# Expert tiles of an encoder block: the order of wide and narrow products, and the place of one wait

## The reference

```
q   = (xb @ w_query).reshape(TB, PH, 2, PEER_QUERY_DIM // 2)
s   = einsum('thpd,hpkd->thpk', q, sub_keys)      # top 16 of 128 keys, twice, for 8 heads
idx, g = best 16 of the 16 x 16 pairs, and their softmax
u = expert_u[idx]
a = gelu(einsum('td,thkd->thk', xb, u))
return einsum('thk,thkd->td', g * a, expert_v[idx])
```

## Time and profile before

| | us |
|---|---|
| median of 3 runs | 932.35 (932.03 to 935.43) |
| the profiled execution | 932.16 |
| its span, first to last instruction | 930.3 |
| TensorE busy (matmul) | 923.0 (99%) |
| TensorE weight loads | 879.0 (94%) |
| DVE / ACT / GpSimd busy | 799.1 / 576.2 / 373.4 |

### The profile page before, as it was taken

One profiled execution on the slowest core, in us unless ns is written; L12 is line 12 of the kernel. 1 busy time (PEld: TensorE's weight loads), 2 busy tenths in 40 slices (PEclk: granted clock), 3 DMA queues, 4 the chain that ended last, 5 costly groups with the idle time before them and its releaser, 6 DMA issues.

```text
span 930.3 us, 20125 instructions
## 1 busy us (share of the span) xinstructions
PE 923.0 (99%) x6652; PEld 879.0 (94%) x6652; DVE 799.1 (86%) x1613; ACT 576.2 (62%) x1069; POOL 373.4 (40%) x222
## 2 busy tenths in 40 slices
PE   9999999999999999999999999999999999999997
PEld 9999889999999999999999999999999999999997
DVE  7988877887799997888989976788998898989886
ACT  6555764655746646888888776655555555555555
POOL 0000000047697787888877877121121222123200
PEclk9999999999999999999999999999999999999999
DMA  8877658666587897999999999999999999999981
GB/s 303 265 232 230 204 179 245 199 223 214 160 246 241 228 258 199 263 287 279 238 258 278 236 245 256 303 387 380 364 358 368 370 382 352 365 356 359 378 276 46
DMA packets 135828, 256.04 MB, mean 275 GB/s; under 512 B 30964, under 2 KB 79988, under 8 KB 135500
## 3 DMA queue, kind: packets, MB, share of 16 engines
q1 hardware_dynamic: 110508, 226.72, 73.7%
q0 software_dynamic: 24816, 27.60, 12.3%
q10 hardware_dynamic: 432, 0.80, 0.3%
HBM read 229.17 MB, written 25.85 MB: 274 GB/s over the span
## 4 chain that ended last, share of the span: by engine, by line
PE 94%; DVE 3%; issue 1%; ACT 1%; DMA 1%; DVEq 0%; ACTq 0%
PE pOO L1524 29%; PE pOO L1532 8%; PE pMM L1532 8%; PE pTT L1836 6%; PE pOO L1836 6%; PE pMM L1836 6%; PE pSS L1836 6%; PE pOO L1533 4%; PE pMM L1533 4%; PE pTT L1837 3%; PE pOO L1837 3%; PE pMM L1837 3%; PE pSS L1837 3%; DVE wlos L975 1%; PE pSS L1598 1%
## 5 line engine op out<-in xcount | busy, mean ns | idle before, releaser
L695 ACT ACTIVATE whis<-raw 128x1024 fp32r<-128x1024 f32 x326 | 343.7, 1056 | 157.5 <-PE pSS L1837 115.9
L670 POOL DMA_INDIRECT g_scratch<-small x117 | 211.4, 1807 | 51.2 <-issue 33.5
L1524 PE MATMUL pOO<-xpair,whis 128*128 128x232 f32 (+1 forms) x1184 | 205.9, 277 | 0.0
L975 DVE TENSOR_TENSOR wlos<-raw,whis 128x1024 fp32r<-128x1024 f32 x155 | 188.2, 1218 | 11.4 <-ACT whis L695 10.4
L1412 DVE TENSOR_TENSOR wlos<-raw,whis 128x1024 fp32r<-128x1024 f32 x125 | 152.9, 1223 | 38.3 <-ACT whis L695 38.0
L1524 PEld LDWEIGHTS pOO<-xpair,whis 128*128 128x128 f32 x1184 | 179.9, 190 | 1.4 <-issue 1.3
L1524 PE MATMUL pOO<-xpair,wlos 128*128 128x232 f32 (+1 forms) x592 | 163.2, 276 | 0.0
L635 POOL TENSOR_TENSOR wlos<-raw,whis 128x1024 fp32r<-128x1024 f32 x30 | 72.0, 2408 | 214.7 <-ACT whis L695 214.6
L1524 PEld LDWEIGHTS pOO<-xpair,wlos 128*128 128x128 f32 x592 | 112.4, 190 | 0.0
L1532 PE MATMUL pMM<-xpair,whis 128*128 128x464 f32 x336 | 109.8, 375 | 0.0
L1532 PE MATMUL pOO<-xpair,whis 128*128 128x464 f32 x336 | 109.0, 375 | 0.0
(11 more groups left out here) (303 smaller groups left out, 2149.0 us busy)
## 6 DMA issues: line engine op xcount, KB each, us to landing
raw<-in_stream SPq DMA_DIRECT2D x199, 512.0 KB, 4.4
raw<-in_vrows SPq DMA_DIRECT2D x128, 512.0 KB, 6.0
a_scratch<-ast SPq DMA_DIRECT2D x128, 116.0 KB, 3.3
held<-a_scratch SPq DMA_DIRECT2D x128, 116.0 KB, 5.7
g_scratch<-ghot SPq DMA_DIRECT2D x32, 256.0 KB, 4.4
G<-g_scratch SPq DMA_DIRECT2D x124, 64.0 KB, 5.3
biasm<-in_bias SPq DMA_DIRECT2D x8, 256.0 KB, 5.6
g_scratch<-small POOLq DMA_INDIRECT x128
```

What stands on the lines that cost most here:

```text
L670: pool.indirect_dma_start(g_dram, bass.IndirectOffsetOnAxis(goff[:, n:n + 1], 0), gval[:, h, k:k + 1], None, compute_op=ALU.add).then_inc( ...
L695: act.activation(whi[s], raw[s][:], ACT.Copy).then_inc(hi_ready, 1)
L975: dve.tensor_tensor(wlo[t % RING], raw[t % RING][:], whi[t % RING].bitcast(F32), ALU.subtract).then_inc(lo_ready, 1)
L1524: last = pe.matmul(dst, st, mv, start=(opening and c == 0 and q == 0), stop=(closing and c == len(terms) - 1 and q == 2))
```

## The change

In the wide U tiles and in the V tiles, all eight wide products are issued first and all eight narrow ones after them. The wait ahead of the tile now asks for the high half only (`hi_ready`), and the wait for the low half (`lo_ready`) stands ahead of the first narrow product. In U tiles that build a part of G, its first two products now come between the wide and the narrow ones. In the last three V tiles each piece has its three wide products ahead of its three narrow ones. The tiles in narrow form keep their products and order. The number of products, their operands and their destinations are the same as before.

```diff
-            def halves_product(bank, terms, opening, closing):
-                last = None
-                both = bank[:, 0:2 * NU].rearrange("p (q n) -> p q n", q=2)
-                for c, (sh, sl, mv) in enumerate(terms):
-                    pe.matmul(both, sh, mv, start=opening and c == 0, stop=False)
-                    last = pe.matmul(bank[:, 0:NU], sl, mv[:, 0, :], start=False, stop=closing and c == len(terms) - 1)
+            def both_halves(bank, s):
+                both = bank[:, 0:2 * NU].rearrange("p (q n) -> p q n", q=2)
+                for c in range(C):
+                    pe.matmul(both, whi[s][:, c, :], xpair[:, :, c, 0:NU], start=c == 0, stop=False)
+
+            def low_products(bank, s):
+                for c in range(C):
+                    last = pe.matmul(bank[:, 0:NU], wlo[s][:, c, :], xpair[:, 0, c, 0:NU], start=False, stop=c == C - 1)
                 return last
...
+                if wide_tile(i):
+                    dst = wide_u[(i - WIDE_FIRST) % 4]
+                    pe.wait_ge(hi_ready, T_U + i)
...
+                    both_halves(dst, s)
+                    if k is not None:
+                        pe.wait_ge(gbanks_free, k + 1 if k >= 2 else 2)
+                        g_tokens(k, 0)
+                    pe.wait_ge(lo_ready, T_U + i + 1)
+                    low_products(dst, s).then_inc(tile_done, 1)
+                    if k is not None:
+                        g_tokens(k, 1)
...
             def v_wait(i):
-                pe.wait_ge(lo_ready, i + (T_V + 1))
+                pe.wait_ge(hi_ready, i + T_V)
                 pe.wait_ge(glo_ready, i + 1)
+            def low_wait(i):
+                pe.wait_ge(lo_ready, i + (T_V + 1))
 
             def v_tile(i, s):
                 v_wait(i)
-                last = None
                 for c in range(C):
-                    last = v_products(i, s, c, c == C - 1 and isinstance(i, int) and i == NE_TILES - BY_BLOCK - 1)
+                    v_both(s, c)
+                low_wait(i)
+                for c in range(C):
+                    last = v_low_products(s, c, c == C - 1 and isinstance(i, int) and i == NE_TILES - BY_BLOCK - 1)
                 last.then_inc(tile_done, 1)
```

More of the change, by code:

```diff
@@ L1802, in _ @@
                 s = (T_U + i) % RING
[L1803 to L1808, removed]
+                if wide_tile(i):
+                    dst = wide_u[(i - WIDE_FIRST) % 4]
+                    pe.wait_ge(hi_ready, T_U + i)
+                    if i < WIDE_FIRST + 2:
+                        pe.wait_ge(evac_act, evac_engine(last_use(T_U + i))[1])
+                    elif i < WIDE_FIRST + 4:
                         pe.wait_ge(gbanks_free, 1)
@@ L1811, in _ @@
                         pe.wait_ge(halves_added, i - 4 - WIDE_FIRST + 1)
[L1812 to L1816, removed]
-                    else:
[L1818 to L1825, removed]
+                    both_halves(dst, s)
[6 more added lines that the diff above has]
+                        g_tokens(k, 1)
+                else:
+                    if i < WIDE_FIRST:
+                        tile_wait(T_U + i)
+                    else:
+                        pe.wait_ge(lo_ready, T_U + i + 1)
+                        pe.wait_ge(halves_added, i - 4 - WIDE_FIRST + 1)
+                    for half in range(1 if k is None else 2):
+                        part = range(C) if k is None else range(half * C // 2, (half + 1) * C // 2)
+                        last = split_product(pO[i % 2][:, 0:NU], [(whi[s][:, c, :], wlo[s][:, c, :], xhi[:, c, 0:NU], xlo[:, c, 0:NU]) for c in part], 0 in part, C - 1 in part)
+                        if C - 1 in part:
+                            last.then_inc(tile_done, 1)
+                        else:
+                            pe.wait_ge(gbanks_free, k + 1 if k >= 2 else 2)
+                        if k is not None:
+                            g_tokens(k, half)
                 if i < 2:
@@ L1830, in _, with v_both, v_low_products, v_end @@
             pe.wait_ge(gbanks_free, 2 + G_STEPS)
-            def v_products(i, s, c, closing=False, dst=None, opening=False):
-                last = None
-                if dst is None:
-                    pe.matmul(wide[c], whi[s][:, c, :], gpair[s], start=opening, stop=False)
-                    return pe.matmul(acc[c][:, 0:NU], wlo[s][:, c, :], ghi[s], start=False, stop=closing)
+            def v_both(s, c, opening=False):
+                pe.matmul(wide[c], whi[s][:, c, :], gpair[s], start=opening, stop=False)
+            def v_low_products(s, c, closing=False):
+                return pe.matmul(acc[c][:, 0:NU], wlo[s][:, c, :], ghi[s], start=False, stop=closing)
+            def v_end(s, opening, closing):
                 for n, (st, mv) in enumerate(((whi, ghi), (whi, glo), (wlo, ghi))):
-                    last = pe.matmul(dst[:, 0:NU], st[s][:, c, :], mv[s], start=opening and n == 0, stop=closing and n == 2)
+                    last = pe.matmul(end7, st[s][:, 7, :], mv[s], start=opening and n == 0, stop=closing and n == 2)
                 return last
             def v_wait(i):
+                pe.wait_ge(hi_ready, i + T_V)
+                pe.wait_ge(glo_ready, i + 1)
+            def low_wait(i):
                 pe.wait_ge(lo_ready, i + (T_V + 1))
-                pe.wait_ge(glo_ready, i + 1)
             def v_tile(i, s):
                 v_wait(i)
-                last = None
                 for c in range(C):
-                    last = v_products(i, s, c, c == C - 1 and isinstance(i, int) and i == NE_TILES - BY_BLOCK - 1)
+                    v_both(s, c)
+                low_wait(i)
+                for c in range(C):
+                    last = v_low_products(s, c, c == C - 1 and isinstance(i, int) and i == NE_TILES - BY_BLOCK - 1)
                 last.then_inc(tile_done, 1)
@@ L1860, in _ @@
                     pe.wait_ge(evac_act, act_takings(T_U) + NE_TILES - 1 + c % 4)
-                last = v_products(0, 0, c, opening=True)
+                v_both(0, c, True)
+            low_wait(0)
+            for c in range(C):
+                last = v_low_products(0, c)
             last.then_inc(tile_done, 1)
@@ L1872, in _ @@
                 v_tile(i, i % RING)
[L1873 to L1876, removed]
-                for i in range(NE_TILES - BY_BLOCK, NE_TILES):
[L1878 to L1883, removed]
+            for i in range(NE_TILES - BY_BLOCK, NE_TILES):
+                v_wait(i)
+                v_both(i % RING, 0)
+            for i in range(NE_TILES - BY_BLOCK, NE_TILES):
+                low_wait(i)
+                v_low_products(i % RING, 0, i == NE_TILES - 1)
+            for c in range(1, C - 1):
+                for i in range(NE_TILES - BY_BLOCK, NE_TILES):
+                    v_both(i % RING, c)
+                for i in range(NE_TILES - BY_BLOCK, NE_TILES):
+                    last = v_low_products(i % RING, c, i == NE_TILES - 1)
                 if c in (1, 3) or c >= 5:
                     last.then_inc(acc_done, 1)
+            pe.wait_ge(h2_ready, 2)
+            for i in range(NE_TILES - BY_BLOCK, NE_TILES):
+                last = v_end(i % RING, i == NE_TILES - BY_BLOCK, i == NE_TILES - 1)
+            last.then_inc(acc_done, 1)
             def turn_out(c, b):
```

## The result

The changed kernel takes 936.98 us (median of 5 runs, 936.41 to 937.95) against 932.35 us before (5 runs beside them). The ratio is 1.0049, with a 95% interval of 1.0031 to 1.0067: 4.6 us slower. The prediction said 927.1 us and faster, with a range of 920.0 to 935.5. It was wrong in sign and just outside its range.

The account below looks back on a forecast made before the run. TensorE's products were taken to bound the kernel. 26.6 ns less on each of 209 tiles gave 5.56 us, plus 0.05 for the last V tiles, less 0.35 for supply: 5.3 us saved, 927.1 us, range 920.0 to 935.5.

Parts of the forecast that it names:

- What bounds the kernel, and the waits: TensorE, busy 99% of the span, sets the time; the moved wait, met 4.8 us ahead, was taken as 0.
- The chain of narrow products at 111.7 ns: Seven narrow products a tile, each behind a narrow one, at 111.7 instead of 106 ns by weight load: plus 39.9 ns.
- the recorded distance behind a wide product: In V before the change, a narrow product's start to the next wide start: 106 ns, taken as its present price.
- the 214 for a wide one: In V before the change, a wide start to the next narrow start: 214 ns, taken as its present price.
- The wide product behind a wide one at 204.5 ns: Seven wide products a tile at 204.5 instead of 214 ns, from two rows behind products for G: minus 66.5 ns.
- a stall of 9.5 ns behind every narrow product: A wide product behind a narrow one was read as standing some 9.5 ns for its weights, hidden behind a long product.
- each product has its own price: Rival, 28%: wide 208.3 ns and narrow 111.7 whatever stands beside them, so the time stays 932.35 us.
- The lower bound of 200: Lowest wide-behind-wide distance, 193.3 + 6.6 ns for 464 columns, from a 256-column chain at 113.3; as a rival 8%, 921.1 us.
- The sum: 26.6 ns less a tile over 209 U and V tiles, 5.56 us, plus 0.05, less 0.35: 5.3 us gained.
- The second one: Rival, 12%: wide products keep 214 ns behind a wide one, the narrow chain slows by 39.9 ns a tile: 940.7 us.
- The first one: Rival, 28%: each product has its own price whatever its neighbours, wide 208.3 ns and narrow 111.7: 932.35 us.
- Supply early in V: In V's first tiles, up to 622.86 us, late weights would take back the 0.35 us that 13 tiles save.

Follow-up runs that it names:

- waits alone: Kernel before with only the change's waits (high half ahead of the tile, low half ahead of the first narrow product), product order as before: 931.57 us, ratio 0.9997.
- order alone: Changed kernel's order, but the low-half wait ahead of the tile as before and none for the high half: 937.61 us, ratio 1.0055.
- v_alt_248: Kernel before, V only: token halves side by side without a gap, narrow products of 248 columns instead of 232, order of before: 936.74 us, ratio 1.0038.
- v_alt_200: Kernel before, V only: token halves side by side without a gap, narrow products of 200 columns instead of 232, order of before: 931.60 us, ratio 0.9988.
- groups of two: Changed kernel with wide U and V tiles issued as wide, wide, narrow, narrow, four times a tile; waits of the change: 937.33 us, ratio 1.0058.
- groups of four: Changed kernel with wide U and V tiles issued as four wide, four narrow, twice a tile; waits of the change: 936.36 us, ratio 1.0058.
- v_grp_232: Kernel before, V only: eight wide then eight narrow products, token halves side by side without a gap, narrow products of 232 columns: 933.96 us, ratio 1.0030.
- v_alt_232: Kernel before, V only: token halves side by side without the 24-column gap, narrow products of 232 columns, order of before: 934.04 us, ratio 1.0027.

## Why the prediction was wrong, point by point

**What bounds the kernel, and the waits: right.** TensorE is the bound before and after, and the moved wait is free, as "waits alone" shows. The row of waits with 1.0 us for DVE is not the cause: "order alone" has none and loses as much.

**The chain of narrow products at 111.7 ns: right** (111.5), and so was the reason given, the load. What I made of it was not clean. I priced it against 106, the recorded distance behind a wide product; by the loads it stands against 108.3, so the true price is 3.2 ns, not 5.7. What I put into the narrow products too much, the 214 for a wide one had too much as well, so this alone moved no sum.

**The wide product behind a wide one at 204.5 ns: wrong, and this is the step that failed.** It measured 212.1. This term was to bring 66.5 ns a tile, and it brought nothing that the loads can see: 211.7 before, 212.1 and its edges after. In the terms of the prediction, by recorded starts, the wide products of a tile were to take 214 + 7 x 204.5 = 1645.5 ns and took 1699.7; the narrow ones were to take 887.9 and took 886.4. The whole error of 54 ns a tile is in the wide ones.

The two rows with 0.20 and 0.21 behind the products for G were real: in the unchanged kernel this wide slot is 204.1 by the loads too, over the 50 of them from 363 to 586 us. But it holds only for a wide product with two G products before it and a narrow one behind it. In the changed kernel the one with G products before it and a wide one behind it takes 212.5 (25 of them). Why the one neighbourhood gives 204 and the other 212 stays open. I read an effect of two neighbours as a stall of 9.5 ns behind every narrow product, and took it for removable. The test was in my own rows: if each wide product lost 9.5 ns, a narrow one would have to cost 115.5 in its place, and the chain showed 111.7. I saw this as the rival "each product has its own price" (wide 208.3, narrow 111.7), gave it 28%, and did not look at the loads' starts, which give 211.7 and 108.3 at once.

**The lower bound of 200: too low.** 464 columns in 212.1 ns are 0.457 ns a column, the chain of 256 columns stood at 113.3 / 256 = 0.443. I took the 6.6 ns over its estimate as a fixed part of each product. With a fixed part the longer product would be the cheaper one for a column, and it is the dearer one. Taken in proportion, 464 x 0.443 = 205.4 would still have been 7 ns too low. The price of a column was not one number in these runs: in v_alt_248 a pair of 712 columns takes 324.5 ns, 0.456, split into 116.7 (0.471) and 207.8 (0.448).

**The sum.** Expected 26.6 ns less a tile, measured 26.5 more: the narrow ones bring 22.6 (seven times 3.2), the wide ones 3.9, of which 2.4 in the row (six times 0.4) and 1.5 at its edges. For the 209 tiles that is 5.5 us; the traces have 5.7 for them and 0.2 for the last three V tiles, where I had expected 0.05 less.

**The rivals.** The second one had the mechanism and the sign: the wide product keeps its price, the chain slows, and it decides above 208.3. It had 12%, and its 940.7 us was too high: it left the wide ones at 214, where they are recorded 212 apart. The first one (28%), 208.3 and 111.7 whatever stands beside them, falls with the narrow slot of 108.3 in the order of before. Of the two rules of the Trainium skill ("TensorE: Matmul & The Clock Gate", "LDWEIGHTS (loading the stationary operand)" and "Back-to-back issue gap") the one for a load, 106.7 ns, lies near the measured 108.3, and the one for a product, which the page gives for a product by itself and not for a stream with loads, makes 195.8 ns of 464 columns, 16 ns below the 212.1 of the chain.

**Supply early in V** took back nothing in particular; waits of 0.4 to 1.0 us turn up there in some executions of either order, and late in V too (v_alt_200, groups of two).

## What to carry to other kernels

Where a product is shorter than a weight load, try a long one between any two of them: here the load was then 108 ns instead of 111.7, 3% of each short product, and grouping by form gave that away. Measure it all the same, since with the token halves side by side the wide products took the gain back. Before using a distance between two products as a price, read the distance between the loads beside it, and check that prices taken from different neighbourhoods add up in the stretch that is already there. A wait that is met microseconds ahead was neither a cost nor a gain here (0.9997 for the waits alone).

## What the runs showed of the hardware

A load of 128 x 128 weights of the fast 32-bit format takes 108.1 to 108.6 ns from its start to the next one where the load before it began over 200 ns earlier, and 110.8 to 111.7 where one short product lay between. That holds for the V loads of all twelve kernels with 200 or 232 columns, the one before and the changed one included, but for the last slot of a chain in two of them (112.5 in the groups of four and 115.1 in v_grp_232). Why the second load is 3 ns dearer no run shows. I had not expected two prices for a load.

Closing a gap of 24 columns between the two halves of a moving operand made the kernel in the order of before 0.27% slower (v_alt_232, 1.0014 to 1.0041), by 2 ns a wide product, where the grouped one had its wide products 1.6 ns shorter. With 200 columns in the same layout the wide one stood at 211.9, so it is not the gap alone. A layout that is not part of a change can move its result by half of what was measured here.
